# Convolution's output product between the half levels of the recurrence's inversion

## The reference

```python
def block3(h):                        # h: (512, 1024)
    h = h + 0.5 * swiglu(rmsnorm(h))
    hn = rmsnorm(h)
    u  = hn @ w_in                    # hyena inputs, gates, rwkv inputs
    yh = hyena(u) @ hy_out            # long convolution, 512 wide, then (512, 1024)
    yr = rwkv7(u) @ rw_out            # delta rule recurrence in both directions, 512 wide
    mixed = sigmoid(gate_h) * yh + sigmoid(gate_r) * yr
    h = h + mixed @ w_out
    h = h + 0.5 * swiglu(rmsnorm(h))
    return rmsnorm(h)
```

## Time and profile before

| | |
|---|---|
| median of 3 runs | 2992.67 us (2992.57 to 2994.12) |
| the profiled execution | 2994.27 us, span 2992.5 us |
| granted TensorE clock | 0.997 of full speed |
| TensorE (PE) busy | 2925.6 us, 98% |
| VectorE (DVE), ScalarE (ACT), GpSimd (POOL) busy | 50%, 36%, 8% |
| rounds k = 0 to 3 of the recurrence (builds) | 2242 to 2499 us |
| rounds k = 4 and 5 | 2499 to 2542 us |
| merge and first units of `mix_out` | from 2542 us |

### The profile page before, as it was taken

How to read it: one execution, slowest core, us unless ns; L and a number is a source line. 1 busy time by engine, 2 the same in 40 slices (tenths; PEclk the granted TensorE clock), 3 DMA queues, 4 the chain that set the end, 5 groups by cost and what they waited for, 6 DMA issues and landing times.

```text
span 2992.5 us, 46857 instructions
## 1 busy us (share of the span) xinstructions
PE 2925.6 (98%) x21214; PEld 2415.7 (81%) x21214; DVE 1486.3 (50%) x1473; ACT 1089.4 (36%) x1179; POOL 234.3 (8%) x134
## 2 busy tenths in 40 slices
PE   8999999999999999999999999999999998999998
PEld 6778878888888888888878888778878887888886
DVE  6665544443454544343454443555667654644432
ACT  5554542222454732222342222442244432332222
POOL 1002110000100010000110000320002220000001
PEclk9999999999999999999999999999999999999999
DMA  4220012223222022222222223222230002222222
GB/s 145 74 72 2 30 71 99 99 95 110 99 94 92 29 82 88 97 99 106 108 89 99 99 100 109 95 78 85 78 116 5 4 6 116 99 90 94 98 100 83
DMA packets 44902, 249.29 MB, mean 83 GB/s; under 512 B 8443, under 2 KB 12283, under 8 KB 17184
## 3 DMA queue, kind: packets, MB, share of 16 engines
q1 hardware_dynamic: 43552, 242.11, 22.7%
q10 hardware_dynamic: 1152, 4.19, 0.3%
HBM read 237.90 MB, written 8.39 MB: 82 GB/s over the span
## 4 chain that ended last, share of the span: by engine, by line
PE 90%; DVE 5%; ACT 3%; issue 2%; POOL 0%; DMA 0%; SPq 0%; DVEq 0%; ACTq 0%; POOLq 0%
PE ps L651 71%; PE ps L2876 7%; PE ps L1492 2%; PE ps L2458 1%; PE ps L2174 1%; PE ps L3935 1%; PE ps L2442 1%; PE ps L3918 1%; ACT whi L266 1%; PE ps L3947 1%; PE ps L2142 0%; DVE wlo L272 0%; DVE gdn_conv L1124 0%; PE ps L3063 0%; PE ps L1655 0%
## 5 line engine op out<-in xcount | busy, mean ns | idle before, releaser
L272 DVE TENSOR_TENSOR wlo<-wraw,whi 128x2048 fp32r<-128x2048 f32 x210 | 486.6, 2318 | 923.3 <-ACT whi L266 921.6
L266 ACT ACTIVATE whi<-wraw 128x2048 fp32r<-128x2048 f32 x210 | 402.1, 1915 | 923.2 <-PE ps L651 923.0
L651 PE MATMUL ps<-ffn_xh,whi 128*128 128x512 f32 x1408 | 553.0, 393 | 0.2 <-DVE wlo L272 0.2
L651 PE MATMUL ps<-ffn_xl,whi 128*128 128x512 f32 x1408 | 550.8, 391 | 0.0
L651 PE MATMUL ps<-ffn_xh,wlo 128*128 128x512 f32 x1408 | 548.3, 389 | 0.0
L651 PEld LDWEIGHTS ps<-ffn_xh,whi 128*128 128x128 f32 x1408 | 264.4, 188 | 59.6 <-DVE wlo L272 1.0
L651 PEld LDWEIGHTS ps<-ffn_xh,wlo 128*128 128x128 f32 x1408 | 264.3, 188 | 58.8
L651 PEld LDWEIGHTS ps<-ffn_xl,whi 128*128 128x128 f32 x1408 | 264.5, 188 | 55.3 <-issue 0.7
L651 PE MATMUL ps<-ffn_uh,whi 128*128 128x512 f32 x704 | 276.0, 392 | 0.0
L651 PE MATMUL ps<-ffn_ul,whi 128*128 128x512 f32 x704 | 275.4, 391 | 0.0
L651 PE MATMUL ps<-ffn_uh,wlo 128*128 128x512 f32 x704 | 274.1, 389 | 0.0
(11 more groups left out here) (520 smaller groups left out, 4686.2 us busy)
## 6 DMA issues: line engine op xcount, KB each, us to landing
wraw<-in_weights SPq DMA_DIRECT2D x211, 1024.0 KB, 4.7
gates_kept<-gates_tmp ACTq DMA_DIRECT2D x8, 512.0 KB, 4.1
mix_gate<-gates_kept SPq DMA_DIRECT2D x8, 512.0 KB, 11.1
h<-in_x SPq DMA_DIRECT2D x4, 512.0 KB, 9.0
mix_y<-hz_kept SPq DMA_DIRECT2D x2, 1024.0 KB, 5.9
out<-out SPq DMA_DIRECT2D x4, 512.0 KB, 3.1
wraw<-in_weights SPq DMA_DIRECT2D x2, 512.0 KB, 7.4
ple_raw<-in_p SPq DMA_DIRECT2D x4, 256.0 KB, 5.1
```

The costliest lines, as they stand in the source:

```text
L266: c.nc.scalar.activation(c.whi[:, j % 2, :], c.wraw[:, j % 2, :], ACT.Copy).then_inc(c.hi_ready, 1)
L272: c.nc.vector.tensor_tensor(c.wlo[:, j % 2, :], c.wraw[:, j % 2, :], c.whi[:, j % 2, :].bitcast(F32), ALU.subtract).then_inc(c.lo_ready, 1)
L651: last = nc.tensor.matmul(pair[:, m, :], a, b, start=opens and n == 0 and wa + xa == 0, stop=closes and n == len(ks) - 1 and wa == 1)
```

## The change

1. The weight tiles of the merge are sorted anew: two tiles with `hy_out` alone, then two with `rw_out` alone.
2. The convolution's output product is issued in the recurrence (`pe_fill`), a quarter of it (256 of 1024 columns) in each build: 24 matmuls, one at the end of each even slot from 10 to 24 and two at the end of each odd slot from 11 to 25. They go to `banks[1]` of `Z_BANK` (first 12) and `F_BANK` (last 12).
3. These banks are free because the right products now write both results into `banks[0]`, XT's into its upper half.
4. The quarter's weights are split from `wraw` straight into a small pair of tiles, by ScalarE and VectorE, in slots 3 and 6 of k = 0 and at the end of rounds 0, 1 and 2.
5. ScalarE copies each half of the result into `staged` (slots 19 and 26), SP stores it in DRAM (`yh_kept`). `pe_turn` waits for these copies.
6. The operands `hz` stand in the place of `c.h`: h goes to DRAM (`h_kept`) early in the convolution's stage, `hz` is loaded before the first build, and h is loaded back after the last fill.
7. When the builds have ended, the four tiles of products and the eight of gates are loaded, 6 MB as before.
8. The merge has 2 weight tiles and 4 groups, all of the recurrence. Its first three row blocks run ahead (12 units: 6, 2, 2, 2 in slots 0, 17, 19, 21). GpSimd multiplies the convolution's product with its gates and makes three of the four low parts.

```diff
-    for c in range(0, DM, WN):
-        plan.append(("hy_out_2|rw_out_2", [(k * P, c, k, 0, P, WN) for k in range(DR // P)]
-                     + [(k * P, c, DR // P + k, 1, P, WN) for k in range(DR // P)]))
+    for w in ("hy_out_2", "rw_out_2"):
+        for c in range(0, DM, 2 * WN):
+            plan.append((w, [(k * P, c + s * WN, s * (DR // P) + k, 0, P, WN) for s in range(2) for k in range(DR // P)]))
...
 class Residual(Dense):
...
+                if q == 0 and self.h_back:
+                    dve.wait_ge(*self.h_back)
...
 class HyenaConv:
...
+            sp.dma_start(self.c.h_kept, self.c.h[:, :, :]).then_inc(self.c.moved, 16)
...
 class Recurrence(Part):
...
     def sync(self, sp):
         c = self.c
+        sp.wait_ge(self.keep.stored, 32)
+        sp.wait_ge(c.moved, 16)
+        for b in range(2):
+            sp.dma_start(self.z[b][:, :, :].bitcast(F32), c.hz_kept[b]).then_inc(self.loaded_back, 16)
         for p in range(2, HP):
             sp.wait_ge(*self.at("lora", 4 * (p - 2) + 3))
             self.load_pair(sp, p, self.wa, self.wa_loaded, 0)
-        for p in range(2, HP):
-            sp.wait_ge(*self.at("g", p - 2))
-            self.load_pair(sp, p, self.gl, self.gl_loaded, 2)
+        for t in range(4):
+            if t >= 2:
+                sp.wait_ge(*self.at("g", t - 2))
+                self.load_pair(sp, t, self.gl, self.gl_loaded, 2)
+            sp.wait_ge(*self.fill_A.at(f"staged{2 * t + 1}"))
+            sp.dma_start(c.yh_kept[t], self.staged[:, :, :]).then_inc(self.keep.stored, 16)
+            if t % 2 == 0:
+                ring_load(c, sp, self.j_held - 2 + t // 2)
+        sp.wait_ge(*self.filled(7))
+        sp.dma_start(c.h[:, :, :], c.h_kept).then_inc(c.moved, 16)
...
+    def pe_fill(self, pe, t, units):
...
+            m, i = divmod(n, 3 * HP)
+            kk, (wa, xa) = i // 3, ((1, 0), (1, 1), (0, 0))[i % 3]
+            if n == 0:
+                pe.wait_ge(*((c.lo_ready, self.j_held + 1 + t // 2) if t % 2 else self.fill_V.at(f"wlo{t}")))
+                pe.wait_ge(self.loaded_back, 48)
+            last = nc.tensor.matmul(c.ps[:, (self.Z_BANK, self.F_BANK)[m][1], :], self.w_out[wa][:, kk, m * P:(m + 1) * P],
+                                    self.z[xa][:, kk, :], start=i == 0, stop=i == 3 * HP - 1)
...
     def tensor(self, pe):
...
+                if build is not None and 10 <= s < 26:
+                    at = 3 * ((s - 10) // 2) + s % 2
+                    self.pe_fill(pe, build, range(at, at + 1 + s % 2))
                 if k == HP + 1 and s in (0, 17, 19, 21):
-                    self.merge.tensor_ahead(pe, 0, {0: 6, 17: 9, 19: 12, 21: 14}[s])
+                    self.merge.tensor_ahead(pe, 0, {0: 6, 17: 8, 19: 10, 21: 12}[s])
...
     def pe_right(self, pe, k, l, d):
...
-                self.both(lambda r: self.columns(self.halved(banks[0])[r, n, :], l),
+                self.both(lambda r: self.columns(self.halved(banks[0], 0)[r, n, :], l),
...
-            last = self.both(lambda r: self.columns(self.halved(banks[1])[r, n, :], l), lambda r: self.Y[r, d, n, :],
+            last = self.both(lambda r: self.columns(self.halved(banks[0], 1)[r, n, :], l), lambda r: self.Y[r, d, n, :],
...
     def pe_turn(self, pe, k, what, banks, name):
         src = what[k % 2]
+        pe.wait_ge(*self.fill_A.at(f"staged{2 * k + (banks is self.F_BANK)}"))
...
     def scalar(self, act):
...
+                if build is not None and s in (19, 26):
+                    self.act_staged(act, build, s // 26)
+                if (k, s) == (0, 3):
+                    self.act_fill_weights(act, 0)
+                if k < 3 and s == SLOTS - 1:
+                    self.act_fill_weights(act, k + 1)
...
     def vector(self, dve):
...
+                if (k, s) == (0, 6):
+                    self.dve_fill_weights(dve, 0)
+                if k < 3 and s == SLOTS - 1:
+                    self.dve_fill_weights(dve, k + 1)
...
 class Merge(Dense):
...
-        body = [[(2 * t + b, True, True, [(b * n + k, b * n + k) for k in range(n)]) for b in range(2)]
-                for t in range(4)]
+        early = [(s, True, False, [(s * n + k, k) for k in range(n - 1)]) for s in range(2)]
+        late = [(s, False, True, [(s * n + n - 1, n - 1)]) for s in range(2)]
+        rest = [(2 + s, True, True, [(s * n + k, k) for k in range(n)]) for s in range(2)]
...
+    def gpsimd(self, pool):
+        nc = self.c.nc
+        pool.wait_ge(*self.y.loaded)
+        for t in range(4):
+            yh = self.y.yh[:, t, :, :]
+            nc.gpsimd.tensor_tensor(yh, yh, self.y.gates[t][:, :, :], ALU.mult).then_inc(*self.Q.done(f"merge.hyena{t}"))
+        for t in range(3):
+            out, a, b = self.low(pool, t)
+            nc.gpsimd.tensor_tensor(out, a, b, ALU.subtract).then_inc(*self.Q.done(f"merge.lo{t}"))
...
```

More of the change, by code:

```diff
@@ L178, in sem, with over_h @@
         return ctx.enter_context(nc.semaphore(name))
-    c.at, c.ring, c.sb, c.sem, c.free = at, ring, sb, sem, []
+    def over_h(name, shape, offset):
+        assert offset + 4 * int(np.prod(shape[1:])) <= 4 * KD * T
+        return put(name, shape, F32R, 4 * 6 * WT + offset)
+    c.at, c.ring, c.sb, c.sem, c.free, c.over_h = at, ring, sb, sem, [], over_h
     place = 0
@@ L2810, in sync, with filled @@
             sp.dma_start(self.gates[n][:, :, :], c.gates_kept[n]).then_inc(self.loaded_back, 16)
-        for j in (self.j_held - 2, self.j_held - 1):
+        for n in range(4, 8):
+            sp.dma_start(self.gates[n][:, :, :], c.gates_kept[n]).then_inc(self.loaded_back, 16)
+        for j in (self.j_held, self.j_held + 1):
             ring_load(c, sp, j)
+    def filled(self, n):
+        return (self.c.tile_done, self.j_held + 1 + n // 4) if n % 4 == 3 else self.fill_E.at(f"filled{n}")
+    def pe_fill(self, pe, t, units):
+        c, nc = self.c, self.c.nc
+        for n in units:
+            m, i = divmod(n, 3 * HP)
[5 more added lines that the diff above has]
+                                    self.z[xa][:, kk, :], start=i == 0, stop=i == 3 * HP - 1)
+            if i == 3 * HP - 1:
+                done = 2 * t + m
+                if done % 4 == 3:
+                    last.then_inc(c.tile_done, 1)
+                else:
+                    last.then_inc(*self.fill_E.done(f"filled{done}"))
@@ new lines, in act_fill_weights @@
+    def act_fill_weights(self, act, t):
+        c, j = self.c, self.j_held + t // 2
+        if t:
+            act.wait_ge(*self.filled(2 * t - 1))
+        act.wait_ge(c.raw_loaded[j % 2], 16 * (j // 2 + 1))
+        cols = slice(t % 2 * WT // 2, (t % 2 + 1) * WT // 2)
+        last = c.nc.scalar.activation(self.w_out[1][:, :, :].rearrange("p k n -> p (k n)"), c.wraw[:, j % 2, cols], ACT.Copy)
+        if t % 2:
+            last.then_inc(c.hi_ready, 1)
+        else:
+            last.then_inc(*self.fill_A.done(f"whi{t}"))
@@ L2815, in gpsimd, with act_staged @@
+    def act_staged(self, act, t, m):
+        act.wait_ge(*self.filled(2 * t + m))
+        if t and m == 0:
+            act.wait_ge(self.keep.stored, 32 + 16 * t)
+        self.c.nc.scalar.activation(self.staged[:, m, :], self.c.ps[:, (self.Z_BANK, self.F_BANK)[m][1], :], ACT.Copy)\
+            .then_inc(*self.fill_A.done(f"staged{2 * t + m}"))
     def gpsimd(self, pool):
@@ L3974, in free, with units, lo_ready @@
+        self.Q.plan([f"merge.hyena{t}" for t in range(4)] + [f"merge.lo{t}" for t in range(3)])
+    def units(self, r):
+        return [unit[:7] + (unit[7] and unit[2],) for unit in super().units(r)]
     def free(self, q):
-        return self.V.at(f"{('hyena', 'rwkv')[q % 2]}{q // 2}")
+        return self.V.at(f"rwkv{q}")
     def pe_closed(self, last, q):
-        last.then_inc(*self.E.done(f"hyena{q // 2}"))
+        last.then_inc(*self.E.done(f"rwkv{q}"))
+    def lo_ready(self, t):
+        return self.V.at("lo3") if t == 3 else self.Q.at(f"merge.lo{t}")
@@ L3997, in vector @@
-            dve.wait_ge(*self.full(t))
-            nc.vector.tensor_tensor(parts[:, 1, :, :], self.y.gates[4 + t][:, :, :], self.pair(2 * t + 1), ALU.mult).then_inc(*self.V.done(f"rwkv{t}"))
+            dve.wait_ge(*(self.full(t // 2) if t % 2 else self.E.at(f"rwkv{t}")))
+            if t:
+                dve.wait_ge(*self.V.at(f"sum{t - 1}"))
+            nc.vector.tensor_tensor(parts[:, 1, :, :], self.y.gates[4 + t][:, :, :], self.pair(t), ALU.mult)\
+                .then_inc(*self.V.done(f"rwkv{t}"))
@@ L4004, in vector @@
[L4004 to L4009 removed]
+            if t == 1:
+                ring_lo(c, dve, self.j0)
+        out, a, b = self.low(dve, 3)
+        nc.vector.tensor_tensor(out, a, b, ALU.subtract).then_inc(*self.V.done("lo3"))
@@ L4011, in m_of @@
+        ring_lo(c, dve, self.j0 + 1)
     def m_of(self, q, k):
```

98 lines of the change are left out of this document (59 added, 39 removed).

## The result

The kernel became slower: 3009.0 us median of 5 runs (3006.12 to 3009.45) against 2993.95 us (5 runs, 2992.57 to 2994.86) for the kernel before, ratio 1.0048 with a 95% interval of 1.0036 to 1.006. The forecast was 2994.6 us with a range of 2984 to 3004, so the result lies 14.4 us above the forecast and outside the range. The forecast was a growth of 1.9 us on a median of 2992.67; by the medians here the growth is 15.0 us. The profiled execution took 3009.34 us, span 3007.5, granted clock 0.996.

A forecast was written before the change was run, and what follows sets the result against it. TensorE, busy 98% of the span, was taken to bound the kernel. Merge and earlier finish -21.2, recurrence +21.1, weights +1.3, shorter merge +0.7 gave +1.9 us on the median 2992.67: 2994.6 us, range 2984 to 3004.

The forecast's parts named there:

- I take 0.165 us a group: Recurrence: price of tile-shape change per group of moved matmuls; 57 of 64 groups pay, 9.4 us.
- The upper bound of 0.3: Recurrence: highest shape-change price allowed, 0.3 us a group, twice the dearest row.
- The gaps: PE waits in the four builds: 12 to 13 us, of which 10.2 us hide moved matmuls; bounds 5 and 14.
- rival 2: Recurrence: waits move and are not filled, up to +12 us, 3005; slower, with worst of third and fourth rivals, 0.26.
- Rival 1: Recurrence: gaps take the groups, shape change nearly free, -7 to -9 us, 2985; nearly all of faster's 0.22.
- The last finish chain: Last pair's finish: fewer units ahead of the gate product, so it and all behind start 0.7 us sooner.
- The merge: Behind the recurrence: 30 units of three matmuls at 0.228 us each go, 20.5 us less.
- the shorter merge: Merge: GpSimd's sharing and the ring's conversion make its first tiles tight, +0.7 us, bounds 0 and 5.
- Rival 3: Merge becomes bound by VectorE and GpSimd, 3 to 5 us, 2998 to 3000; milder part 0.06, worst within slower's 0.26.
- The three splits of weights between the builds: Ends of builds: half conversions fit with 0.2 us to spare, 0.5 us given; with the first pair's 0.8, +1.3.
- The transfers: SP's queue: added stores and loads have no late reader, zero cost; without that cover 7 us.
- product in the builds, gross: Recurrence: 96 moved matmuls at 0.228 us, 21.9 us, plus 9.4 us of shape changes, 31.3 us in all.

The follow-up runs named there:

- e1: The changed kernel with the four gate products on VectorE inside the merge in place of GpSimd: 3007.29 us median, ratio to before 1.004.
- e2: The changed kernel with only the last of each 12 moved matmuls, 8 of 96, most of the product left out: 2981.72 us, one run.
- e3: The changed kernel with three moved matmuls at each odd slot and none at even ones, 32 groups for 64: 2998.22 us median, ratio to before 1.0011.
- e4: The changed kernel with the moved matmuls on 256 of 512 columns, half the product left out: 3001.15 us, one run.
- e5: e3 with the four gate products on VectorE where it waits, in place of GpSimd: 2993.99 us median of 11, ratio to before 1.0001.

## Why the prediction was wrong

**The step that failed: "I take 0.165 us a group".** Measured is 0.30 to 0.36. Of the seven behind products of 512 columns, for which I took nothing, five pay 0.20 and two, with 128x128 tiles ahead, nothing. By the same sum, 42.5 us gross instead of 31.3: +11.2 us. The upper bound of 0.3 was too low as well. The rows were there. In the earlier trace rows I counted what the neighbours of the larger product lost, 0.12 ahead and 0.045 behind, and took the product's own 1.06 us as its pace. But two such instructions take 0.95 us where a product of 32x128 tiles follows (2572.34 to 2573.29 in after), so 0.11 us of leaving stood inside the row. From 2475.67 to 2477.79 is 2.12; less 0.93 and 0.95 that is 0.24, and with the 0.045 behind 0.29. Had I read the price from the start of the product before to the start of the one after, and not as two edges, I would have taken 0.29 us a group, and the forecast would have been near 3002.

**The gaps gave more than the forecast had:** 12.6 us hidden instead of 10.2, -2.4 us. I had counted 12 to 13 us of gaps rightly (12.5 by starts) and then let only part of them be filled. All four builds hid more than was thought (3.9, 4.2, 2.8 and 1.7 against 3.1, 3.5, 2.2 and 1.4). Of rival 2 (waits that move and aren't filled) nothing is seen: PE idles for 0.09 us in the four stretches. Rival 1 had this half right and failed at its other half, the free change of shape.

**The last finish chain: +3.3 us where the forecast had -0.7.** I had seen GpSimd's effect on VectorE and charged it to the merge, where I thought that the gate products would run. They run as soon as their loads have landed, 5 us before the recurrence ends, and the chain of the last finish is what they meet. The -0.7 itself was right (e1: -0.6); the place of the contention was not, and costs +3.9. Without this the result would still have been some 10 us above the forecast.

**What was right.** The merge: -20.5 forecast without the part that runs ahead, -20.1 measured with the 0.3 us wait at 2580.48, so the +0.7 that I gave for the shorter merge was +0.4. Rival 3 didn't come: in its first tiles the output product doesn't wait. The three splits of weights between the builds are free: from z to slot 10, 28.59, 29.66 and 25.17 us before and 28.58, 29.63 and 25.15 after. I had 0.5 for them. The first pair's cost 0.63; I had 0.8. The transfers cost nothing by themselves (e2 has them all), though their landing sets when GpSimd starts.

| term | forecast | measured |
|---|---|---|
| merge, with the +0.7 | -19.8 | -20.1 |
| product in the builds, gross | +31.3 | +42.5 |
| hidden in gaps | -10.2 | -12.6 |
| last finish chain | -0.7 | +3.3 |
| weights | +1.3 | +0.6 |
| sum | +1.9 | +13.7 |

The sum leaves 1.3 us of the 15.0, ahead of the recurrence (scatter, as said), and 1.3 of the 14.4 above the forecast are the median of before, 2993.95 here against 2992.67.

**What stays open:** why a lone matmul between tiles of another shape costs 0.33 us. The rows show where it lies (0.10 ahead, 0.1 at the first, 0.1 behind the last), that it depends on neither number nor columns, and that it goes away where the product ahead has the same shape, and no more. The fall of the clock goes with the wait in every trace here, but no run changes the wait alone. Behind PE's waits of 3.39, 3.79, 3.53 and 3.08 us (after, e2, e3, e4) the mean granted clock up to the transposes was 0.69, 0.72, 0.69 and 0.56, and that stretch took 5.43, 5.12, 5.46 and 6.54 us. In e1 and e5, without the long wait, it was 1.00 and 4.82 and 4.81 us.

## What to carry to other kernels

Work that is moved into the gaps of a loop with another tile shape pays for each group and not only for each matmul: 0.33 us here, more than the matmul itself. So put it in few groups, each right ahead of a wait or behind a product of its own tile shape, and read the price from start to start across the whole foreign product, not from its edges. Work on GpSimd that has nothing to wait for but a load starts when the load lands: ask what VectorE is doing then, and whether that is the chain that sets the end.

## What the hardware showed that I had not expected

- A float32r matmul of 128x128 by 512 columns between 64x64 products: 0.56 us for one, 0.76 for two, 1.02 for three, 1.72 for six; of 256 columns 0.44 for one. That is 0.30 to 0.35 us plus 0.228 for each 512 columns. Behind a float32 product of 128x128 tiles the 0.3 us are not paid: 0.46 us for two, 1.38 for six.
- VectorE operations of two SBUF operands beside a run of GpSimd multiplies: 1.89 and 2.74 us instead of 0.69. For 128x1024 in e1, 3.42 instead of 1.22.
- Behind a wait of 3.39 us PE's mean granted clock was 0.56 from 2564.30 to 2567.70, so mostly the lower of its two levels (1.2 GHz against 2.4), and a matmul took about 0.43 instead of 0.228 us. Behind a wait of 0.17 us (e1) the clock was 1.00. The last chain became 0.6 us longer in this part.
